# Layer norms by halves of the tokens, their lo parts on GpSimd, in a two-block fp32 network on one core

## The reference

```
def layer_norm(x, g, b):
    mu = jnp.mean(xf, -1, keepdims=True)
    var = jnp.mean(jnp.square(xf - mu), -1, keepdims=True)
    return ((xf - mu) * lax.rsqrt(var + EPS_2) * g + b).astype(x.dtype)

for l in range(2):
    x = layer_norm(ALPHA * x + swiglu_half(x, w1, w3, w2), ln1_g, ln1_b)   # norm 0
    h = x @ w_in[l]                       # D_IN columns: spatial gating, delta rule, linear attention
    mix = concatenate([out_a, out_b, out_c]) @ w_out[l]
    x = layer_norm(ALPHA * x + mix, ln2_g, ln2_b)                          # norm 1
    x = layer_norm(ALPHA * x + swiglu_half(x, w1, w3, w2), ln3_g, ln3_b)   # norm 2
```

## Time and profile before

| | us |
|---|---|
| median of 3 runs (2946.86 to 2949.47) | 2947.76 |
| profiled execution, its own time | 2946.4 |
| its span, first to last instruction | 2944.5 |
| TensorE busy (97% of the span) | 2869.1 |
| VectorE busy (40%) | 1184.2 |
| ScalarE busy (38%) | 1124.5 |
| GpSimd busy (28%) | 827.1 |
| mean granted TensorE clock | 0.988 of full |

### The profile page before, as it was taken

The page is one execution under the profiler, slowest core; times in us unless marked ns, Lnnn a source line. Parts: engine busy times, 40 slices in busy tenths (PEclk is TensorE's granted clock), DMA queues, the critical chain, the costliest instruction groups (busy, mean ns, idle before and its releaser), DMA issues.

```text
span 2944.5 us, 48520 instructions
## 1 busy us (share of the span) xinstructions
PE 2869.1 (97%) x20000; PEld 2370.7 (81%) x20000; DVE 1184.2 (40%) x1484; ACT 1124.5 (38%) x1312; POOL 827.1 (28%) x312
## 2 busy tenths in 40 slices
PE   8999999999999999999999999999999999999997
PEld 6787887787888888788788887888888788788886
DVE  3655653632223243544622324322252543632315
ACT  3557554422323245532333323333245532333224
POOL 4122213411001635361001153100534362010053
PEclk9999999999999999999999999999999999999999
DMA  5111112222222332201122232222332200122233
GB/s 181 44 67 70 58 44 72 82 90 88 100 100 87 142 110 101 73 2 45 62 95 100 100 138 94 100 100 100 129 115 102 80 2 31 58 100 100 100 129 115
DMA packets 36533, 257.63 MB, mean 87 GB/s; under 512 B 4080, under 2 KB 4128, under 8 KB 6432
## 3 DMA queue, kind: packets, MB, share of 16 engines
q1 hardware_dynamic: 34848, 249.66, 23.7%
q0 software_dynamic: 1536, 5.83, 0.6%
HBM read 253.31 MB, written 2.16 MB: 87 GB/s over the span
## 4 chain that ended last, share of the span: by engine, by line
PE 91%; DVE 4%; issue 2%; ACT 2%; POOL 2%; DMA 0%; ACTq 0%; DVEq 0%; POOLq 0%
PE ps L2274 50%; PE ps L1774 6%; PE ps L1729 5%; PE ps L1766 4%; PE ps L2408 3%; PE ps L2460 3%; PE ps L1073 2%; PE ps L2319 2%; PE ps L1059 1%; PE ps L1860 1%; POOL wl L1379 1%; PE ps L1845 1%; PE ps L1831 1%; PE ps L1784 1%; ACT wh L1985 1%
## 5 line engine op out<-in xcount | busy, mean ns | idle before, releaser
L1379 POOL TENSOR_TENSOR wl<-raw,wh 128x2048 fp32r<-128x2048 f32 x114 | 523.6, 4593 | 700.8 <-ACT wh L1985 700.5
L2274 PE MATMUL ps<-xh,wh 128*128 128x512 f32 x1584 | 621.1, 392 | 7.7 <-DVE wl L2095 4.8
L2274 PE MATMUL ps<-xl,wh 128*128 128x512 f32 x1584 | 616.8, 389 | 0.0
L2274 PE MATMUL ps<-xh,wl 128*128 128x512 f32 x1584 | 616.5, 389 | 0.0
L1985 ACT ACTIVATE wh<-raw 128x2048 fp32r<-128x2048 f32 x224 | 427.5, 1908 | 378.4 <-PE ps L2274 309.7
L2095 DVE TENSOR_TENSOR wl<-raw,wh 128x2048 fp32r<-128x2048 f32 x112 | 286.0, 2553 | 555.0 <-ACT wh L1985 552.4
L1950 POOL TENSOR_TENSOR hl<-hf,hh 128x1024 f32 x44 | 105.8, 2404 | 969.9 <-ACT hh L1995 969.9
L2274 PEld LDWEIGHTS ps<-xh,wh 128*128 128x128 f32 x1584 | 297.3, 188 | 80.9 <-issue 8.6
L2274 PEld LDWEIGHTS ps<-xh,wl 128*128 128x128 f32 x1584 | 297.4, 188 | 61.8
L2274 PEld LDWEIGHTS ps<-xl,wh 128*128 128x128 f32 x1584 | 297.4, 188 | 60.6
L2274 PE MATMUL ps<-hh,wh 128*128 128x512 f32 x704 | 276.9, 393 | 1.6 <-POOL wl L1379 1.2
(11 more groups left out here) (375 smaller groups left out, 4597.9 us busy)
## 6 DMA issues: line engine op xcount, KB each, us to landing
raw<-stream SPq DMA_DIRECT2D x232, 1024.0 KB, 4.8
btw<-bias_rows POOLq DMA_DIRECT2D x2, 1536.0 KB, 8.3
x<-x_in SPq DMA_DIRECT2D x4, 512.0 KB, 5.5
out<-x SPq DMA_DIRECT2D x4, 512.0 KB, 2.6
sgp<-sg POOLq DMA_DIRECT2D x2, 640.0 KB, 4.2
cst<-consts SPq DMA_DIRECT2D x1, 1108.0 KB, 9.1
c<-bias_consts SPq DMA_DIRECT2D x1, 1024.0 KB, 14.7
bt<-bias_rows POOLq DMA_DIRECT2D x2, 512.0 KB, 9.1
```

The source lines that it names most:

```text
L1379: nc.gpsimd.tensor_tensor(wl[:, p, :], raw[:, p, :], wh[:, p, :].bitcast(F32), ALU.subtract).then_inc(s["chunk_lo"], 1)
L2274: mm = te.matmul(dst, wslice(w, k), r(k), start=(start and m == 0), stop=(stop and m == len(steps) - 1))
```

## The change

Every norm of the second block is done in two halves of the tokens, 0 to 255 (early) and 256 to 511 (late).

- `down`: tile 7 is multiplied as two halves of 256 tokens each, in two banks (`last_tile`), with the order first chunk early, first chunk late, sums, second chunk early, then the second chunk's late half with the early half's column sums and spreading between its matmuls. The mixer's tiles 6 and 7 are split likewise.
- VectorE adds tile 7 in two halves, takes the column steps twice on two columns each, and centres and scales 16 half tiles instead of 8 tiles; it writes no lo parts of `x` any more. The late half's evacuation, the two halves of the second weight chunk and the late column steps stand between early half tiles.
- ScalarE writes hi part and `x` of 16 half tiles, GpSimd writes the lo parts (`low_parts`, 16 subtractions of 256 tokens, fp32).
- `first_two`: 192 matmuls of 256 tokens: all early halves for both chunks (the second chunk two feature tiles behind the first), with the late column sums after tile 2 and the late spreading after tile 5, then all late halves. `busy` is gone. In the block ahead of the second block's first layer, GpSimd's lo parts are also made by halves.
- At norm 1, VectorE adds the squares 1 to 3 ahead of tile 4; tiles 6 and 7 are left out of the running sums and summed by column instead.
- First norm of the kernel: VectorE adds the squares up (7 additions of 128x512), TensorE sums the one outcome by token (8 instructions), and the lo parts of h tiles 2, 4 and 6 go to VectorE.
- TensorE's program of the two layers is written out twice instead of a hardware loop; the other engines keep theirs.

```
             def first_two(l, off, w, ahead):
...
+                for k in range(KT):
+                    pe.wait_ge(s["early_parts"], parts + k + 1)
+                    products(0, k, 0)
+                    if ahead and k == 2:
+                        late_columns(*ahead)
+                    if k >= 2:
+                        second(k - 2)
+                    if ahead and k == 5:
+                        late_wide(*ahead)
+                second(6)
+                second(7)
+                for p in range(2):
+                    for k in range(KT):
+                        if p == 0:
+                            pe.wait_ge(s["x_parts"], parts + k + 1)
+                        products(p, k, 1)
...
+            def low_parts(l, w):
+                n = l * 3 + w
+                for h in range(2):
+                    t = tokens_of(h)
+                    for k in range(KT):
+                        pool.wait_ge(s["ln_x"] if h else s["early_x"], n * 8 + k + 1)
+                        gp.tensor_tensor(xl[:, k, t], x[:, k, t], xh[:, k, t].bitcast(F32), ALU.subtract)...
...
 ScalarE, norm:
+                root(0)
+                parts(0, 0)
+                half(chunk, 0)
+                parts(1, 0)
+                late_square(l, w, 7, lates)
+                parts(2, 0)
+                half(chunk, 1)
+                parts(3, 0)
+                parts(4, 0)
+                root(1)
+                for k in range(5, KT):
+                    parts(k, 0)
                 for k in range(KT):
+                    parts(k, 1)
...
 first block:
-            for k in range(KT):
-                pe.wait_ge(s["sq_x"], k + 1)
-                for t in range(4):
-                    mm = te.matmul(ps[:, 5, t:t + 1], bsq[:, X_SLOT[k % 4], t * P:(t + 1) * P], mean_matrix[:, 0:1], ...)
+            pe.wait_ge(s["ms_x"], KT - 1)
+            for t in range(4):
+                mm = te.matmul(ps[:, 5, t:t + 1], bsq[:, 2, t * P:(t + 1) * P], mean_matrix[:, 0:1], ...)
```

More of the change, by code:

```diff
@@ L234 @@
     "x_in3": "tiles 6 and 7",
+    "rms_columns": "mean squares by token",
+    "h_low": "the lo part of a tile of h that VectorE makes",
     "rrms_wide": "the reciprocals over all partitions",
@@ L256 @@
     "out_early_x": "tile 4, then tile 6 is added to x",
-    "ln_mean": "mean of the shifted tiles, over all partitions",
+    "late_x": "the second half of the tokens of tile 7 (and of the mixer's tile 6) is added to x",
+    "half_lo": "VectorE has written the lo part of that half",
+    "early_down": "the first half of these tiles is in PSUM",
+    "early_square": "its square",
+    "early_columns": "mean and mean square of the first two token tiles",
+    "early_column": "VectorE's steps on these",
+    "early_std": "their root",
+    "early_wide": "mean and 1 / std over all partitions, first two token tiles",
+    "early_centred": "the first half of a tile, centred",
+    "early_scaled": "times gain / std",
+    "early_x": "with the bias, back in x",
+    "early_parts": "both parts of the first half of a tile",
     "half_hi": "ScalarE has rounded the first half of the chunk after a norm",
@@ L2051, in down @@
                 root_table(l)
-                half(n + 15, 0)
-                squares(l, w, (7,), evicted)
-                half(n + 15, 1)
-                norm(l, w)
+                evicted(7)
+                early_squares(l, w, (7,))
+                norm(l, w, n + 15, 1)
             block1_act(act, round_chunk)
@@ L2354, in down, with last_tile @@
                         shift(l, w)
-                    if f == 7:
-                        sums(l, w)
                     down_half(l, w, f, f % 2, 1, off)
-                busy(4)
-                pe.wait_ge(evac[1], n_evac(l, 1, off) + KT)
+                n = c_no(l, off) + 14
+                pe.wait_ge(evac[1], n_evac(l, 1, off) + 6)
+                pe.wait_ge(s["ln_shifted"], (l * 3 + w) * 8 + 8)
+                pe.wait_ge(s["z_sum"], z_no(l, w) + 6)
+                def last_tile(p, h, ks=range(11)):
+                    c = tokens_of(h)
+                    for k in ks:
+                        for a, (w_, r) in enumerate(((wh, hh), (wh, hl), (wl, hh))):
+                            mm = te.matmul(ps[:, 4 if h else 2, c], w_[:, p, k * P:(k + 1) * P], r[:, 11 * p + k, c],
+                                           start=(p == 0 and k == 0 and a == 0), stop=(p == 1 and k == 10 and a == 2))
+                    return mm
@@ L2397, in first_two, with early_columns @@
-            def first_two(l, off, ready):
+                added = 8 if w == 1 else 9
+                pe.wait_ge(s["z_sum"], z_no(l, w) + added)
+                for h in range(2):
+                    by_token(h, 0, zacc, True, False)
+                pe.wait_ge(s["ln_square_sum"], sq_no(l, w) + added - 3)
+                for h in range(2):
+                    by_token(h, 1, sqacc, False, False)
+            def early_columns(l, w, tiles):
+                pe.wait_ge(s["early_square"], late_no(l, w) + len(tiles))
+                for k in tiles:
+                    by_token(0, 0, x[:, k, :], False, False)
+                    mm = by_token(0, 1, sqt[:, k % 2, :], False, k == 7)
+                mm.then_inc(s["early_columns"], 1)
@@ L2402, in first_two, with products @@
                 pe.wait_ge(s["chunk_lo"], n + 1)
-                def products(p, k):
+                parts = l * 24 + w * 8
+                def products(p, k, h):
+                    t = tokens_of(h)
                     for j in range(2):
                         c = 256 * k + P * j
-                        for a, (w, r) in enumerate(((wh, xh), (wh, xl), (wl, xh))):
-                            mm = te.matmul(ps[:, 2 * p + j, :], w[:, p, c:c + P], r[:, k, :], start=(k == 0 and a == 0), stop=(k == KT - 1 and a == 2))
-                    if k == KT - 1:
+                        for a, (w_, r) in enumerate(((wh, xh), (wh, xl), (wl, xh))):
+                            mm = te.matmul(ps[:, 2 * p + j, t], w_[:, p, c:c + P], r[:, k, t], start=(k == 0 and a == 0), stop=(k == KT - 1 and a == 2))
+                    if k == KT - 1 and h:
@@ L2453, in out_steps @@
                         pe.wait_ge(s["rec_state"], l * 9 + 9)
+                    regions = [(OUT_BANK[t], slice(0, 512))] if t < 6 else [(LATE_BANK[t] if half else OUT_BANK[t], tokens_of(half)) for half in halves]
+                    if n == OUT_HALVES.index((0, 6)):
+                        pe.wait_ge(evac[0], n_evac(l, 0, OFF_OUT) + 1)
                     for kk in ks:
@@ L2488, in _ @@
                 out_half(11, (2, 3))
-                for n in (12, 13, 14):
+                for n in (12, 13):
                     out_half(n)
-                out_half(15, (0, 1))
+                for m, half in ((14, 0), (15, 0), (14, 1)):
+                    for _ in out_steps(m, halves=(half,)):
+                        pass
                 sums(l, 1)
-                out_half(15, (2, 3))
-                busy(4)
-                pe.wait_ge(evac[1], n_evac(l, 1, OFF_OUT) + 2)
-                norm(l, 1)
-                first_two(l, OFF_UP2, normed(l, 2))
+                early_columns(l, 1, (6, 7))
+                for _ in out_steps(15, halves=(1,)):
+                    pass
+                early_wide(l, 1)
+                first_two(l, OFF_UP2, 2, (l, 1))
                 with pe.Fori(1, UP // 2) as i:
```

317 lines of the change are left out of this document (189 added, 128 removed).

## The result

The changed kernel takes **2966.35 us** (median of 4 runs, 2964.45 to 2967.05), the kernel before on the same chip 2947.32: a ratio of **1.0062, 95% interval 1.005 to 1.0075**. It is slower by 19 us, where the forecast of about 2953 was 5.7 over the same time, and it lies outside the range (up to 2963).

The account below looks back on a forecast made before the run. TensorE, busy 97% of the span, was taken as the bound. Start -6.3, norm 0 +8.0, norm 1 0, layer change +.6, last norm +2.3 made +4.6 (+4.8 with norm 1's .1s): about 2953 us, range 2937 to 2963.

Parts of the forecast that it names:

- Norm 1, "0 each": At norm 1 of each layer, step to third chunk: 48.5 us against 48.4 before, so no change.
- The wait of 4.74 goes, because the sums no longer hold tile 6.: At norm 1, TensorE's wait of 4.74 us for VectorE's sums was to disappear.
- For the clock I take 2.6: At norm 1, 2.6 us allowed for lower clock, more than at norm 0: longer wait, sixteen one-column matmuls following.
- Norm 0, +4.0 each: Norm 0 of both layers, T0 (last tile's products start) to third chunk: 53.6 us against 49.6 before.
- The clock allowances: Time added at the norms for TensorE's lower clock; 2.6 us at norm 1, more than at norm 0.
- the clock stays down: Rival, chance .20: five broken stretches each run 3.4 us more at half speed, +8.5 in all, giving 2961.
- the supply runs ahead: Rival, chance .15: half tiles pass between engines faster, the inner waits of 4.2 us go, giving 2925.
- The layer change, +.6: Between the layers, GpSimd's later parameter fetch makes T0 to third chunk 56.3 us against 55.7.
- The last norm, +2.3: At the last norm, ScalarE's last write of x ends 41.4 us after T0 against 39.15.
- The start, -6.3: At the kernel's first norm, the root starts at 13.4 us instead of 19.69; what follows shifts with it.

Follow-up runs that it names:

- Run 3: Changed kernel with norm 1's weight-chunk lo parts back on VectorE behind the squares, tiles 4 and 5 added ahead of the squares: 2967.47 us, ratio 1.0068.
- run 5: Changed kernel with norm 1's chunk lo parts back on VectorE and filler matmuls in every wait of a norm: 2947.05 us, ratio .9998.
- run 1: Changed kernel with filler matmuls put back: 10, 6, 4 before tiles 0, 1, 2, and 12 before norm 1's sums: 2951.20 us, ratio 1.001.
- run 2: Kernel before without its filler matmuls (4 and 12 at every norm): 2966.34 us, ratio 1.0068.
- run 8: Kernel before with only the first norm's squares added on VectorE, measured twice: 2945.76 us (ratio .9994) and 2945.29 us (.9997).
- run 6: Changed kernel, no filler, with one-column matmuls issued one at a time between products: 2974.49 us, ratio 1.009.
- runs 2 and 7: Run 7: kernel before with each matmul of the first two chunks after each norm place split into two of 256 tokens: 2958.11 us, ratio 1.0036.

## Why the prediction was wrong

The side was right, the size was not: +19.0 instead of +5.7.

**Norm 1, "0 each" (+5.3 and +6.9): the step that failed.** It failed in two places.
- *"The wait of 4.74 goes, because the sums no longer hold tile 6."* It did not; 2.80 and .41 were left. I asked what the sums need and not what stands in front of it on VectorE, where the change put three additions of squares ahead of tile 4, while GpSimd, newly given a subtraction of 4.60, blocked the first of them. Run 3 shows that undoing this order alone moves the wait on to the squares and columns. In run 5, with this order undone and no half clock, the first parts still come 17.8 after the step where I had 14.4: 3.4 us of waits that the forecast has not.
- *"For the clock I take 2.6."* From the step at 1417.70 the first parts were forecast after 14.4 and came after 20.1. Of the 5.7, 3.2 are the waits above; 24 one-column records took 4.6 instead of 2.8 and 12 halves 2.7 instead of 1.45, 3.1 of clock; the forecast's own work was .6 too long. Behind the first parts the total was right by two errors: 32.7 against 32.8, with waits of .7 instead of 4.1, and clock where the waits should have been. Run 5, with the clock up and the waits filled, gives 56.2 against the 56.0 of before: my 0 is what this norm costs at full speed and no better, though I had put 2.6 of clock into it. Clock and order together then cost 5.2 and 7.0 in the changed kernel; run 1's fillers alone bring 4.0 and 4.7 of it back.

**Norm 0, +4.0 each (+4.8, +4.0).** The number held, its parts did not. The first parts came 21.7 after T0 (22.3 forecast); then 25.2 of work took 31.4, of which 1.5 are waits (4.2 forecast) and the rest, 4.7, is clock by subtraction (1.0 forecast). Run 1 gives only 2.5 and 1.8 of that back, since at full clock a new wait of .98 for GpSimd's lo parts appears. So the number held by luck: waits too high by 2.7 beside a clock too low by 3.7. With filler everywhere norm 0 still costs 2.2 to 2.7 over before: 162 pairs at .0135 are 2.2 of it.

**The clock allowances** are thus mis-sized at all five places. I had them as 1.0 (run 1 gave back 2.5 and 1.8), 2.6 (4.0 and 4.7) and nothing at the layer change (2.7), bounded by what a single wait had cost in the kernel before. The mechanism was named ("the filler is gone") and priced from the wrong rows: the earlier trace rows are from a kernel that still had its filler. What it keeps off was not in the trace of before at all; run 2 shows it, 9.4 at the norm places. Of the rivals, *the clock stays down* was the right one and near its size: with my own allowances it put 2.0 + 5.2 + 8.5 = 15.7 on the clock, which is what run 1 gave back. Its 2961 is short of 2966 by about what norm 1's forecast misses at full clock, 2.5 at each of two; *the supply runs ahead* held for the waits (1.5 and .7 instead of 4.2) and brought nothing, as TensorE ran slower instead.

**The layer change, +.6 (+.4),** held by luck. GpSimd's last lo part was forecast to end about 46 after T0 and did so at 45.9, but behind 10.2 us of TensorE at half clock, where the forecast had waits. With the clock up (run 1) the fetch is issued at 44.1 instead of 46.6, and the third chunk starts 53.3 after T0, 2.4 under before.

**The last norm, +2.3,** was +.9: late spreading ended at 32.1 after T0, not 33, and ScalarE's half tiles came .85 apart, not .93.

**The start, -6.3,** held in the trace (-6.2) and failed in the kernel's time: run 8 shows the start's gain arrive and all but 1.0 to 1.4 of it leave again in the mixers. I assumed that unedited code takes the time it took.

**What stays open.** Why the wait behind the mixer's loop comes and goes with edits elsewhere; that it follows from where TensorE's instructions come to lie is a guess, which no run tested. The changed kernel has such waits too (.62 and 1.13). Norm 1's share of order and of clock was not taken apart at full clock.

## What to carry to other kernels

Before removing matmuls that compute nothing, run the kernel without them: the trace that has them cannot show what they are for. In the changed kernel, putting such matmuls back into the waits brought 15 us of the 19 lost; in the kernel before, taking them out cost 20, half of it away from the norms. When a wait is broken into several short ones, fill them all: the longest alone gave 10.0 of 15.7 us at the norm places, and 5 to 6 of 15 in the kernel's time. And halving a matmul's columns to start earlier cost .009 to .0135 us a pair here, against a gain that must be shown at full clock.

## What the runs showed of the hardware

- The granted clock fell to half right behind waits of 2.15 and 1.02 us with six products of 256 columns between them, and stayed there for 10.2 us while TensorE was busy for 9.7 of them. With short matmuls spread among the products it stayed down for 34 us (run 6); 20 records of 128 columns in a wait of 2.4 us, 12 and 8 more behind tiles 0 and 1, kept it up (run 1).
- A VectorE addition of two SBUF operands took 4.2 us instead of .69 beside GpSimd's subtraction of 4.60; a VectorE step with one operand in PSUM took its usual .68 beside it.
- A wait of 1.4 to 2.0 us in straight code on TensorE, released by no engine, appeared in four mixers of four when only the start was edited (28 fewer one-column matmuls, over 1300 us earlier). The four mixers of the unchanged kernel have at most one of .38; those of runs 2 and 7, with edits at the norms alone, have 1.1 to 1.9.
- With no edit between them, two profiles of one kernel differ by 3 us in one mixer, with 6.8 us more at half clock.
